# Dilated attention computed by classes of tokens modulo four: 64 by 64 blocks, two heads at a time

## The chip, the cores and the metric

One core of one Trainium2 chip runs the whole program. The metric is the device time of one execution in microseconds (us), lower is better; the kernel before was run three times.

## The reference, cut to what matters

Everything is float32. The program is two transformer blocks one after the other over 256 tokens of width 1024. The change touches one layer of the first block, dilated attention, and the tables that it reads:

```
B_WINDOWS = (128, 512, 2048)
B_DILATIONS = (1, 4, 16)
B_HEADS = 16;  B_HEAD_DIM = 64;  SEQ = 256
...
biases = [rel_bias[bucket][..., g * B_HEADS:(g + 1) * B_HEADS] ... for g ...]
...
s = einsum('birhd,bjrhd->bhrij', qb, kb) + biases[g]     # queries and keys of equal residue r only
s = where(valid, s, -inf)                                # distance in 0..window, not before token 0
p = exp(s - logsumexp(s));  o = einsum('bhrij,bjrhd->birhd', p, vb)
...
wts = softmax(stack(lses), axis=0)                       # over the three groups
o = einsum('gbqh,gbqhd->bqhd', wts, stack(outs));  return o @ w_o
```

There are three groups of 16 heads each. In group g a query attends to the keys whose distance is a multiple of the dilation: every key for group 0 (window 128), every fourth for group 1, every sixteenth for group 2. Weighting the three outputs by the softmax of their log sums is the same as one softmax over the keys of all three groups together, and the kernel computes it that way: one row of probabilities per query and head, over three stretches of keys. The bias depends on the head, the group and the distance.

## The kernel before, in words

The program is a series of stages: a feed-forward stage, a gated recurrence (`hgrn`, the reference's `_hgrn2`), another feed-forward stage, `dil` (the dilated attention), and so on. In the profiled execution `hgrn` runs from about 233 to 357 us, the feed-forward stage after it to 727, and `dil` to about 1027.

**Weights.** SyncE (queue q1, "SPq") loads each weight slice into `raw`. ScalarE copies it rounded to `whi` (L1304), VectorE computes the rest `wlo` (L1724), and TensorE multiplies by both. Only a few buffers of `raw` exist, so a load goes out when an earlier one has been read, and it is needed some microseconds later.

**Slots.** A stage with projections is cut into slots. A slot of `dil` is one product of 48 matmuls (L793 to L795 for q and v, L814 to L816 for k; also L793 for a part). Heads go in four units of four heads. A unit has nine slots: q and k for three groups (six slots), then v for three groups. The q and k slots are scaled by VectorE into `dl_t` (L1768), squared by ScalarE, summed by TensorE (L1011, L1012) and normalized. Values go through VectorE into `dl_v` (L1786).

**Attention steps.** The attention of one unit is laid into the slots of the next one, at half-slot points listed in four tables. TensorE takes the steps in the order of its program, and while it does one of them, no projection runs:

```
DL_SCORES = (13, 14, 16, 18)
DL_SCALE = (14, 15, 17, 19)
DL_TURN = (15, 17, 19, 21)
DL_PV = (19, 22)
```

For each head of a unit: SCORES (TensorE, L1056) multiplies 128 queries by 256 keys and the first 128 queries by 128 keys, for the three groups, where one head or group takes rows 0 to 63 of the array and another rows 64 to 127; VectorE adds the bias and takes the maximum (L2010); ScalarE takes the exponential (L1533) in place in `dl_S` (128 x 1152 for a head); SCALE divides by the sum (L2002 on VectorE, L2293 on GpSimd); TURN transposes nine 128 x 128 pieces (L1039) and ScalarE copies them to `dl_PT` (L1528). PV (L1024) multiplies by the values of two heads, one in columns 0 to 63 of the array, the other in 64 to 127; its result goes to `dl_oT` (L1523). Blocks of groups 1 and 2 are computed as densely as those of group 0: the bias of a distance that is not allowed is a large negative number.

**Bias tables.** The bias by distance is made in `hgrn`, where TensorE multiplies a table of zeros and ones by `rel_bias` (L994) at ticks 8, 10 and 12, ScalarE copies the result to `bias_rows` (L1496) a tick later, and ScalarE's queue (q10, "ACTq") stores it to DRAM many times over, each time shifted by a row, so that a later load finds a skewed table. Twelve stores (L1423), one for each tick from 10 on and the last three together in the last tick, each read all 128 partitions. A tick is one slot of `hgrn`: 16 ticks of projections and four of the output product (L883 to L885). Before `dil` ScalarE's queue waits for all stores, and then loads the bias of each head (L1507) two heads ahead, right after the head's exponentials.

Of the kernel before, what the change touches and what calls it, by code (L numbers as in the profile page):

```python
# [18 lines left out]
ALU = mybir.AluOpType  # L19
# [6 lines left out]
P = 128  # L26
# [22 lines left out]
SWAPPED = 1  # L49
# [16 lines left out]
def t5_bucket(dist):  # L66
# [8 lines left out]
    ("neg_mask", P), ("hg_mask", (LEVELS - 1) * P), ("swa_mask", T), ("cos", T), ("sin", T), ("onehot", GROUPS * 3 * P),  # L75
# [9 lines left out]
def constants():  # L85
# [36 lines left out]
    onehot = np.zeros((BUCKETS + 1, GROUPS, 3 * P), np.float32)  # L122
    dist = T - 1 - np.arange(3 * P)
    for g, (w, dil) in enumerate(zip(WINDOWS, DILATIONS)):
        valid = (dist >= 0) & (dist <= w) & (dist % dil == 0)
        bucket = t5_bucket(np.maximum(dist, 0))
        onehot[bucket[valid], g, np.nonzero(valid)[0]] = 1.0
        onehot[BUCKETS, g] = ~valid
# [4 lines left out]
def build_program(nc, io, upto=None):  # L133
# [87 lines left out]
    ROW = 3 * P  # L221
    REPEAT = P // HEADS
    BIAS_STORES = 4 * GROUPS
    spare = ExitStack()
    bias_rows = sb("bias_rows", [P, GROUPS, ROW], F32, spare)
    rbx = sb("rbx", [BUCKETS + 1, GROUPS * HEADS], F32, spare)
    rbx8 = sb("rbx8", [BUCKETS + 1, GROUPS * P], F32, spare)
    onehot = sb("onehot", [BUCKETS + 1, GROUPS * ROW], F32, spare)
# [64 lines left out]

    bias_dram = nc.dram_tensor("bias_by_distance", (GROUPS * HEADS * P * ROW,), F32, kind="Internal").ap()

# [90 lines left out]

    def r_of(e):

        return r[:, e % 2:e % 2 + 1, :].broadcast_to([P, 2, T])
# [63 lines left out]
    HG_BIAS = 8  # L453
# [53 lines left out]

    region = ExitStack()
# [3 lines left out]
    dl_v = sb("dl_v", [P, 2, GROUPS, T // P, 4 * HD], F32, region)  # L512
    dl_bias = sb("dl_bias", [P, 2, GROUPS, T], F32, region)
    dl_S = sb("dl_S", [P, 2, 3 * GROUPS * P], F32, region)
    dl_PT = sb("dl_PT", [P, 2, 3 * GROUPS * P], F32, region)
# [23 lines left out]
    DL_SCORES = (13, 14, 16, 18)  # L539
    DL_SCALE = (14, 15, 17, 19)  # L540
    DL_TURN = (15, 17, 19, 21)
# [23 lines left out]
    def dl_blocks(ap, keys):  # L565

        at0 = 0 if keys == T else GROUPS * T
        return ap[:, at0:at0 + GROUPS * keys].rearrange("p (g k) -> p g k", g=GROUPS)

    dl_ps = ps[:, DL_BANK:DL_BANK + 3, :].rearrange("p b n -> p (b n)")[:, 0:3 * GROUPS * P]  # L570

    def dl_paired(hd):

        return hd < HEADS - 2

    def dl_scores(hd, keys):

        at0, bank = 0 if keys == T else T, DL_BANK + (hd % 2 and dl_paired(hd))
        return ps[:, bank:bank + GROUPS, at0:at0 + keys]

    def dl_rows(a, g):

        odd = (a + (g == SWAPPED)) % 2
        return slice(HD * odd, HD * (odd + 1))
# [191 lines left out]
    def _(pe):  # L776
# [133 lines left out]
        def hgrn():  # L910
# [56 lines left out]
            for t in range(HG_TICKS):  # L967
# [20 lines left out]
                if t in HG_BIAS_AT:  # L988
# [3 lines left out]
                    else:  # L992
                        pe.wait_ge(bias_masked, 2)
                    nc.tensor.matmul(ps[:, HG_BIAS_BANK, 0:ROW], rbx8[:, P * g:P * (g + 1)], onehot[:, ROW * g:ROW * (g + 1)],  # L994
                                     start=True, stop=True).then_inc(bias_made, 1)


        def dil():
            st, e, ek = stages["dil"], reads["dil"], reads["dil"] - 1

            def steps(point):
# [11 lines left out]
                for two in dl_due(point, DL_PV):  # L1013
# [1357 lines left out]
```

## Time and profile before

| | us |
|---|---|
| median of 3 runs | 2165.11 |
| lowest and highest run | 2163.71, 2165.37 |
| span of the profiled execution | 2161.0 |
| TensorE busy, of the span | 2126.5 (98%) |
| VectorE busy | 1607.5 (74%) |
| ScalarE busy | 1307.3 (60%) |
| one unit of `dil`, 840.30 to 909.05 | 68.75 |

The profile gives no time of the profiled execution other than its span, from the first to the last instruction: the median of the runs is 4.1 us above it. "Busy" is the time in which an engine had an instruction under way. TensorE has two rows in every view: PE are the matmuls, PEld the loads of their weights, which run beside the matmul before. A float32 matmul that is not of rounded operands leaves two records. The column PEclk is the granted clock of TensorE, 1.00 being full.

### The profile page before, as it was taken

To read this page: it belongs to the slowest core of one execution; us is meant where nothing else is said; L and a number is where in the kernel's file an instruction comes from. 1 tells how busy PE (TensorE), PEld (TensorE's weight loads), DVE (VectorE), ACT (ScalarE), POOL (GpSimd) and SP (SyncE) were. 2 spreads that over 40 slices of the span, in tenths; PEclk is the share of its full clock that TensorE was granted. 3 is DMA by queue.
4 is the path that set the end of the run, shared out by engine and by line. 5 is a ranking of instruction groups with operands and counts; after the bars stand their busy time and mean duration, and the time that the engine had idled before them with its cause. 6 is when DMAs were issued, how large, how long until landed. Compare 5 with 4: busy or idle time off the path is not lost.

```text
span 2161.0 us, 39632 instructions
## 1 busy us (share of the span) xinstructions
PE 2126.5 (98%) x14203; PEld 1920.3 (89%) x14203; DVE 1607.5 (74%) x1915; ACT 1307.3 (60%) x1815; POOL 586.1 (27%) x450
## 2 busy tenths in 40 slices
PE   8999899999999999999999999999999999999998
PEld 7889899888888899999888888999888888888887
DVE  7875888886887676766887687665887688677874
ACT  6664776664665565665665566475665466456663
POOL 3431672440342000000442243000342144122430
PEclk9999999999999999999999999999999999999999
DMA  6665467666566555554566567544566566534673
GB/s 211 193 199 180 128 191 259 193 209 189 166 194 212 165 172 162 160 160 150 168 194 211 158 194 220 159 145 149 177 192 212 158 191 202 187 108 150 191 221 100
DMA packets 371157, 387.92 MB, mean 180 GB/s; under 512 B 11334, under 2 KB 366031, under 8 KB 371056
## 3 DMA queue, kind: packets, MB, share of 16 engines
q1 hardware_dynamic: 357104, 369.14, 54.9%
q10 hardware_dynamic: 13952, 17.41, 2.5%
q8 instruction: 66, 1.08, 0.2%
q14 instruction: 35, 0.29, 0.0%
HBM read 376.02 MB, written 10.49 MB: 179 GB/s over the span
## 4 chain that ended last, share of the span: by engine, by line
PE 90%; DVE 5%; ACT 3%; POOL 1%; issue 1%; DMA 0%; ACTq 0%; DVEq 0%
PE ps L839 44%; PE ps L840 23%; PE ps L793 3%; PE ps L794 3%; PE ps L795 3%; PE ps L814 2%; PE ps L815 1%; PE ps L816 1%; DVE xg L1742 1%; PE ps L883 1%; DVE wlo L1724 1%; PE ps L885 1%; PE ps L884 1%; PE ps L1056 1%; PE ps L1024 1%
## 5 line engine op out<-in xcount | busy, mean ns | idle before, releaser
L1724 DVE TENSOR_TENSOR wlo<-raw,whi 128x1024 fp32r<-128x1024 f32 (+2 forms) x652 | 883.1, 1364 | 153.7 <-ACT whi L1304 152.6
L839 PE MATMUL ps<-xg,whi 128*128 128x512 f32 x2816 | 981.8, 392 | 4.1 <-DVE xg L1742 1.9
L1304 ACT ACTIVATE whi<-raw 128x1024 fp32r<-128x1024 f32 (+2 forms) x652 | 720.6, 1113 | 190.5 <-PE ps L840 130.2
L840 PE MATMUL ps<-xg,wlo 128*128 128x256 f32 x2816 | 794.5, 282 | 0.0
L839 PEld LDWEIGHTS ps<-xg,whi 128*128 128x128 f32 x2816 | 529.2, 188 | 118.3 <-DVE xg L1742 3.9
L840 PEld LDWEIGHTS ps<-xg,wlo 128*128 128x128 f32 x2816 | 532.9, 189 | 0.2
L839 PE MATMUL ps<-hT,whi 128*128 128x512 f32 x1408 | 488.5, 390 | 0.0
L840 PE MATMUL ps<-hT,wlo 128*128 128x256 f32 x1408 | 397.1, 282 | 0.0
L839 PEld LDWEIGHTS ps<-hT,whi 128*128 128x128 f32 x1408 | 264.3, 188 | 55.4
L2235 POOL TENSOR_TENSOR gate_r<-gate,r 128x512 f32<-128x512 f32 x88 | 189.6, 2155 | 286.5 <-DVE gate L1802 286.5
L840 PEld LDWEIGHTS ps<-hT,wlo 128*128 128x128 f32 x1408 | 266.1, 189 | 0.0
L793 PE MATMUL ps<-xg,whi 128*128 128x256 f32 x576 | 164.7, 286 | 3.2 <-DVE wlo L1724 3.2
L794 PE MATMUL ps<-xg,whi 128*128 128x256 f32 x576 | 160.8, 279 | 0.0
L2240 POOL TENSOR_TENSOR hT<-h,hT 128x512 f32 x88 | 117.3, 1333 | 159.8 <-ACT hT L1357 159.8
L795 PE MATMUL ps<-xg,wlo 128*128 128x256 f32 x576 | 160.6, 279 | 0.0
L2238 POOL TENSOR_TENSOR gate_s<-gate_r,gate_s 128x512 f32<-128x512 f32 x88 | 114.9, 1306 | 155.9 <-ACT gate_s L1351 155.9
L1820 DVE SCALAR_TENSOR_TENSOR x<-ps,x 128x512 f32<-128x512 f32 x32 | 22.1, 692 | 157.1 <-PE ps L840 157.1
L1346 ACT ACTIVATE gate_e<-gate 128x512 f32<-128x512 f32 x88 | 55.7, 633 | 137.2 <-DVE gate L1802 137.2
L1806 DVE TENSOR_SCALAR gate_e<-gate_e 128x512 f32<-128x512 f32 x88 | 129.6, 1472 | 5.6 <-ACT gate_e L1346 5.6
L2227 POOL TENSOR_TENSOR acc<-acc,sq 128x512 f32<-128x512 f32 x13 | 18.2, 1401 | 369.9 <-ACT sq L1316 369.9
L793 PEld LDWEIGHTS ps<-xg,whi 128*128 128x128 f32 x576 | 108.3, 188 | 7.0 <-issue 4.9
L1311 ACT ACTIVATE xg<-x,gains 128x256 fp32r<-128x256 f32 x96 | 43.4, 500 | 110.2 <-DVE x L1822 102.1
(286 smaller groups left out, 3067.2 us busy)
## 6 DMA issues: line engine op xcount, KB each, us to landing
raw<-in_ffn_w_in SPq DMA_DIRECT2D x352, 512.0 KB, 3.5
raw<-in_ffn_w_out SPq DMA_DIRECT2D x64, 768.0 KB, 4.7
raw<-in_ffn_w_out SPq DMA_DIRECT2D x64, 640.0 KB, 4.7
raw<-in_w_kv SPq DMA_DIRECT2D x48, 512.0 KB, 3.6
raw<-in_a_w_in SPq DMA_DIRECT2D x32, 512.0 KB, 4.5
raw<-in_b_w_q SPq DMA_DIRECT2D x24, 512.0 KB, 3.8
raw<-in_sb_w_qkv SPq DMA_DIRECT2D x24, 512.0 KB, 3.9
bias_by_distance<-bias_rows ACTq DMA_DIRECT2D x12, 768.0 KB, 5.0
```

Of the source, the lines that this page charges most:

```text
L793: nc.tensor.matmul(out, whi[:, par, w], hi[:, k, :], start=k == 0 and m == 0, stop=False)
L794: nc.tensor.matmul(out, whi[:, par, w], lo[:, k, :], start=False, stop=False)
L795: mm = nc.tensor.matmul(out, wlo[:, par, w], hi[:, k, :], start=False, stop=k == total - 1 and m == 1)
L839: nc.tensor.matmul(out, whi[:, par, w], both, start=first and k == 0, stop=False)
L840: mm = nc.tensor.matmul(out[:, 0:T], wlo[:, par, w], both[:, 0:T], start=False, stop=last and k == total - 1)
L1304: nc.scalar.activation(whi[:, par, off:off + size], raw[:, 2 * par + half, :size], ACT.Copy).then_inc(hi_done, 1)
L1346: nc.scalar.activation(gate_e[:, :], gate[:, :], ACT.Exp, scale=-1.0).then_inc(gate_exp, 1)
L1724: nc.vector.tensor_tensor(wlo[:, par, off:off + size], raw[:, 2 * par + half, :size], whi[:, par, off:off + size].bitcast(F32), ALU.subtra ...
L1806: nc.vector.tensor_scalar(gate_e[:, :], gate_e[:, :], EXP_MAX, 1.0, ALU.min, ALU.add).then_inc(gate_den, 1)
L2235: nc.gpsimd.tensor_tensor(pair(gate_r[:, :]), pair(gate[:, :]), r_of(e), ALU.mult).then_inc(gr_done, 1)
L2238: nc.gpsimd.tensor_tensor(gate_s[:, :], gate_r[:, :], gate_s[:, :], ALU.mult).then_inc(gs_done, 1)
L2240: nc.gpsimd.tensor_tensor(hidden(i, 1), pair(h[:, :]), hidden(i, 0).bitcast(F32), ALU.subtract).then_inc(hT_ready, 1)
```

## The change

The tokens of a product that belongs to `dil` are written in order of their class modulo four: first tokens 0, 4, 8, ..., then 1, 5, 9, ... A group with dilation 4 or 16 then has all its allowed pairs inside four blocks of 64 by 64. Group 0 still takes 128 queries by 256 keys, now for both tiles of queries, since its class order mixes early and late tokens. A head's row of probabilities shrinks from 1152 columns of `dl_S` (768 and 384) to 768 (two tiles of 384). Groups 1 and 2 are computed as 64 x 64 matmuls in one of the four quadrants of the array, two heads together. Steps come two heads at a time.

The tables of steps, and the VectorE step for the values of groups 1 and 2 (one call in each of their slots, in place of `scaled_values`):

```
-    DL_SCORES = (13, 14, 16, 18)
-    DL_SCALE = (14, 15, 17, 19)
-    DL_TURN = (15, 17, 19, 21)
+    DL_SCORES = (13, 17)
+    DL_SCALE = (14, 18)
+    DL_TURN = (16, 20)
     DL_PV = (19, 22)
...
+        def class_values(g, u, fill):
+
+            for tile in range(2):
+                for half in range(2):
+                    rows, out = slice(HD * half, HD * (half + 1)), slice(HD * (g - 1), HD * g)
+                    op = nc.vector.tensor_scalar(dl_w[out, u % 2, 2 * tile + half, :], bank_of(fill)[rows, W2 * tile:W2 * (tile + 1)],
+                                                 r_col[rows, tile:tile + 1], None, ALU.mult)
+            op.then_inc(evac_done, 1)
```

PV:

```
-                    for g in range(GROUPS):
-                        for tile in range(2):
-                            for odd in range(2):
-                                v = dl_v[:, u % 2, g, tile, HD * (2 * c + odd):HD * (2 * c + odd + 1)]
-                                at0, n = (T * g, T) if tile == 0 else (GROUPS * T + P * g, P)
-                                mm = nc.tensor.matmul(ps[HD * odd:HD * (odd + 1), DL_OUT, T * (c + 1) - n:T * (c + 1)], v,
-                                                      dl_PT[:, odd, at0:at0 + n], start=g == 0 and tile == 0 and c == 0,
-                                                      stop=g == GROUPS - 1 and tile == 1, tile_position=(0, HD * odd), skip_group_check=True)
+                    for tile in range(2):
+                        for odd in range(2):
+                            v = dl_v[:, u % 2, tile, HD * (2 * c + odd):HD * (2 * c + odd + 1)]
+                            nc.tensor.matmul(ps[HD * odd:HD * (odd + 1), DL_OUT, T * c:T * (c + 1)], v, dl_PT[:, odd, T * tile:T * (tile + 1)],
+                                             start=c == 0 and tile == 0, stop=False, tile_position=(0, HD * odd), skip_group_check=True)
+                    for kind in range(CLASSES):
+                        at0 = OF_CLASS * kind
+                        for odd in range(2):
+                            w = dl_w[:, u % 2, kind, HD * (2 * c + odd):HD * (2 * c + odd + 1)]
+                            mm = nc.tensor.matmul(ps[HD * odd:HD * (odd + 1), DL_OUT, T * c + at0:T * c + at0 + OF_CLASS], w,
+                                                  dl_PT[:, odd, 2 * T + at0:2 * T + at0 + OF_CLASS], start=False, stop=kind == CLASSES - 1,
+                                                  tile_position=(0, HD * odd), skip_group_check=True)
```

SCORES, the part for groups 1 and 2, and the order of a pair's steps:

```
+                    def far(hds, tile):
+
+                        for g in range(1, GROUPS):
+                            for half in range(2):
+                                for hd in hds:
+                                    rows, at0 = dl_rows(hd), T * c + OF_CLASS * (2 * tile + half)
+                                    bank = DL_BANK if dl_split(hd, tile) else DL_BANK + 2 * (hd % 2) + 1 - tile
+                                    cols = (DL_TILE if dl_split(hd, tile) else dl_far(tile)) + OF_CLASS * (g - 1)
+                                    mm = nc.tensor.matmul(ps[HD * half:HD * (half + 1), bank, cols:cols + OF_CLASS],
+                                                          dl_q[rows, g, at0:at0 + OF_CLASS], dl_k[rows, u % 2, g, at0:at0 + OF_CLASS],
+                                                          start=True, stop=True, tile_position=(rows.start, HD * half))
...
+                    if odd < HEADS - 1:
+                        for tile in (1, 0):
+                            near(even, tile)
+                            near(odd, tile)
+                        far((even, odd), 1)
+                        far((even, odd), 0).then_inc(dl_scored, 2)
```

The stores and the loads of the bias tables:

```
-            def store_bias(g, quarter):
-
-                rows = REPEAT // 2
-                act.dma_start(bass.AP(bias_dram.tensor, HEADS * P * ROW * g + rows * ROW * quarter, [[4 * rows * ROW, P], [ROW, rows], [1, ROW]]),
-                              bias_rows[:, g:g + 1, :].broadcast_to([P, rows, ROW])).then_inc(bias_stored, 16)
+            def store_bias(at0, row, first, head, step):
+
+                act.dma_start(bass.AP(bias_dram.tensor, first, [[head, HEADS], [step, OF_CLASS], [1, row]]),
+                              bias_rows[0:HEADS, at0:at0 + row].unsqueeze(1).broadcast_to([HEADS, OF_CLASS, row])).then_inc(bias_stored, 16)
...
+    HG_STORE_AT = (12, 13, 14)
...
-                src = bass.AP(bias_dram.tensor, hd * P * ROW + P - 1, [[ROW - 1, P], [HEADS * P * ROW, GROUPS], [1, T]])
-                act.dma_start(dl_bias[:, hd % 2, :, :], src).then_inc((dl_bias_in0, dl_bias_in1)[hd % 2], 16)
+                arrived = (dl_bias_in0, dl_bias_in1)[hd % 2]
+                for block in range(2):
+                    near = bass.AP(bias_dram.tensor, hd * NEAR_HEAD + P * (1 + 2 * block) + OF_CLASS - 1,
+                                   [[NEAR_ROW - 1, P], [P, CLASSES], [1, OF_CLASS]])
+                    act.dma_start(dl_bias[:, hd % 2, DL_TILE * block:DL_TILE * block + T].rearrange("p (k j) -> p k j", k=CLASSES),
+                                  near).then_inc(arrived, 16)
+                far = bass.AP(bias_dram.tensor, FAR_TABLE + hd * FAR_HEAD + OF_CLASS - 1, [[FAR_STEP - 1, P], [P, 2], [1, OF_CLASS]])
+                act.dma_start(dl_bias[:, hd % 2, T:T + P].rearrange("p (g x) -> p g x", g=2), far).then_inc(arrived, 16)
```

The four stores carry as much as the twelve did, 9.4 MB: two of 16 x 64 x 896 words (3.67 MB each, at ticks 12 and 13, in pieces of 3584 bytes) and two of 16 x 64 x 256 words (1.05 MB each, at tick 14, in pieces of 1024 bytes). They read 16 partitions, one for each head. VectorE's read of the q and k products and of their factors, its and ScalarE's writes of `dl_oT`, and the writes of k's operand in the stage before are now strided.

Three places of the program's order bear on what follows. The first is TensorE in a slot of `dil`, k's product (L814 to L816) with the SCORES of one pair of heads in it and the first PV and TURN of a pair, before (`ps<-dl_k,dl_q` are SCORES, `ps<-cst,dl_S` TURN, `ps<-dl_PT,dl_v` PV):

```order
L816 MATMUL ps<-whi,xk_lo 128x256
L1056 MATMUL ps<-dl_k,dl_q 128x256 x2
L1056 MATMUL ps<-dl_k,dl_q 128x128 x2
L1056 MATMUL ps<-dl_k,dl_q 128x256 x2
L1056 MATMUL ps<-dl_k,dl_q 128x128 x2
...
L1056 MATMUL ps<-dl_k,dl_q 128x256 x2
L1056 MATMUL ps<-dl_k,dl_q 128x128 x2
...
L1039 MATMUL ps<-cst,dl_S 128x128 x9
```

In the changed program the same place reads as follows, up to its first TURN:

```order
L863 MATMUL ps<-whi,xk_lo 128x256
L1111 MATMUL ps<-dl_k,dl_q 128x256 x4
L1121 MATMUL ps<-dl_k,dl_q 64x64 x16
...
L1093 MATMUL ps<-cst,dl_S 128x128 x2
L1094 MATMUL ps<-cst,dl_S 128x128
L1093 MATMUL ps<-cst,dl_S 128x128 x2
L1094 MATMUL ps<-cst,dl_S 128x128
L1093 MATMUL ps<-cst,dl_S 128x128 x2
L1094 MATMUL ps<-cst,dl_S 128x128
L1093 MATMUL ps<-cst,dl_S 128x128 x2
L1094 MATMUL ps<-cst,dl_S 128x128
```

The second head's scores have moved up into the first head's step, twelve dense matmuls have become four dense ones and sixteen small ones, and two times nine transposes at two points have become twelve at one. The second place is PV on TensorE, before and then after:

```order
L1024 MATMUL ps<-dl_PT,dl_v 64x256 x2
L1024 MATMUL ps<-dl_PT,dl_v 64x128 x2
L1024 MATMUL ps<-dl_PT,dl_v 64x256 x2
L1024 MATMUL ps<-dl_PT,dl_v 64x128 x2
L1024 MATMUL ps<-dl_PT,dl_v 64x256 x2
L1024 MATMUL ps<-dl_PT,dl_v 64x128 x2
```

```order
L841 MATMUL ps<-xg,whi 128x256
L842 MATMUL ps<-xg,wlo 128x256
L1072 MATMUL ps<-dl_PT,dl_v 64x256 x4
L1078 MATMUL ps<-dl_PT,dl_w 64x64 x8
L840 MATMUL ps<-xk_hi,whi 128x256
```

Six dense pairs have become two dense pairs and four of 64 columns. The third place is ScalarE in `hgrn`, the copies of a table (L1496) and the stores that it issues. Before, from tick 11 on:

```order
L1304 ACTIVATE whi<-raw 128x1024
L1423 DMA bias_by_distance<-bias_rows 128x4x384
L1304 ACTIVATE whi<-raw 128x1024 x2
L1407 ACTIVATE newton<-ps,eps 128x256
L1409 ACTIVATE newton<-newton 128x256
L1485 ACTIVATE hg_v<-ps,r_col 128x256 x2
L1496 ACTIVATE bias_rows<-ps 128x384
L1423 DMA bias_by_distance<-bias_rows 128x4x384
L1304 ACTIVATE whi<-raw 128x1024 x2
```

In the changed program:

```order
L1572 ACTIVATE hg_v<-ps,r_col 128x256 x2
L1584 ACTIVATE bias_rows<-ps 128x384
L1506 DMA bias_by_distance<-bias_rows 16x64x896
L1388 ACTIVATE whi<-raw 128x1024 x2
...
L1506 DMA bias_by_distance<-bias_rows 16x64x896
L1388 ACTIVATE whi<-raw 128x1024 x2
...
L1584 ACTIVATE bias_rows<-ps 128x256
L1506 DMA bias_by_distance<-bias_rows 16x64x256 x2
```

No store goes out before tick 12 any more, and none after tick 14; all 9.4 MB are in ScalarE's queue within three ticks.

## Rows read from the trace of the kernel before

**Rows 1.** The page: busy time of each engine; the chain that ended last.
```profile
PE 2126.5 (98%) x14203; PEld 1920.3 (89%) x14203; DVE 1607.5 (74%) x1915; ACT 1307.3 (60%) x1815; POOL 586.1 (27%) x450
...
PE 90%; DVE 5%; ACT 3%; POOL 1%; issue 1%; DMA 0%; ACTq 0%; DVEq 0%
```
**Rows 2.** Windows: start:end, length, busy PE, PEld, DVE, ACT, POOL, clock, DMA share, GB/s.
```profile
297.00:331.00 34.00, 34.00 (x405) 32.38 (x404) 32.87 (x65) 25.91 (x45) 23.17 (x32) 1.00 0.66 215
331.00:357.00 26.00, 24.89 (x206) 24.37 (x206) 20.16 (x32) 14.62 (x24) 3.72 (x4) 1.00 0.84 278
357.00:726.00 369.00, 368.54 (x2124) 326.19 (x2123) 282.35 (x280) 221.97 (x292) 116.66 (x74) 1.00 0.62 194
...
840.30:909.05 68.75, 68.48 (x578) 64.28 (x578) 48.78 (x71) 43.12 (x63) 3.31 (x4) 1.00 0.54 162
```
**Rows 3.** The chain, one unit of dil: start, us on the chain, what.
```profile
840.29 1.51 PE ps L1056 x16
841.80 0.32 PE ps L814
842.83 0.12 PE ps L815
...
844.84 0.85 PE ps L1056 x8
845.69 0.32 PE ps L814
...
848.77 1.17 PE ps L1039 x9
...
874.69 0.98 PE ps L1039 x9
...
878.95 2.10 PE ps L1024 x24
881.05 0.32 PE ps L793
```
**Rows 4.** The chain in hgrn: small matmuls of 32 columns in pairs.
```profile
303.69 0.82 PE ps L953 x24
...
304.77 0.61 PE ps L953 x22
```
**Rows 5.** Groups of instructions by shape, 726 to 1030: busy, mean ns, idle before.
```profile
L2002 DVE TENSOR_SCALAR dl_S<-dl_S,dl_rcp 128x768 f32<-128x768 f32 x16 | 20.6, 1287 | 0.6
L1528 ACT ACTIVATE dl_PT<-ps 128x1152 f32<-128x1152 f32 x16 | 17.8, 1113 | 0.0
L1786 DVE TENSOR_SCALAR dl_v<-ps,r_col 128x256 f32<-128x256 f32 x24 | 10.5, 478 | 3.0 <-PE ps L816 2.8
```
**Rows 6.** DMA, 285 to 365: queues with packets, MB and share; issues.
```profile
q1 hardware_dynamic: 6842, 9.84, 39.0%
q10 hardware_dynamic: 6334, 9.44, 33.4%
```
**Rows 7.** The instructions that name bias_rows: issue ns, first and last; time to landing.
```profile
L1423 ACTq DMA_DIRECT2D bias_by_distance<-bias_rows x12: 366/366/1137, 287.8 to 352.0; - x12
...
DMA to landing us min/median/max: 3.5/5.0/13.4
```
**Rows 8.** ScalarE in the timeline, 297 to 307: a store, then a weight load awaited.
```profile
298.98 0.37 ACTq L1423 DMA_DIRECT2D bias_by_distance<-bias_rows  x1
...
304.98 1.06 ACT L1304 ACTIVATE whi<-raw 128x1024 fp32r<-128x1024 f32 x1 [3.65 <-DMA raw<-in_a_w_in]
```
**Rows 9.** The instructions of L1507, the bias loads of dil: issue, time to landing.
```profile
L1507 ACTq DMA_DIRECT2D dl_bias<-bias_by_distance x16: 366/366/512, 727.1 to 986.2; - x16
...
DMA to landing us min/median/max: 3.2/3.6/4.8
```

More of the change, by code:

```diff
@@ L563, in dl_qk_number, with dl_heads, dl_probs, dl_near @@
         return 2 * GROUPS * u + min(j, 2 * GROUPS)
[L565 to L584, printed above, removed]
+    def dl_heads(point, steps):
+        return [hd for two in dl_due(point, steps) for hd in (2 * two, 2 * two + 1)]
+    def dl_probs(ap, tile):
+        return ap[:, 0:DL_TILE] if tile else ap[:, DL_TILE:2 * DL_TILE]
+    def dl_near(tile):
+        return 0 if tile else P
+    def dl_far(tile):
+        return T if tile else 0
+    def dl_split(hd, tile):
+        return hd == HEADS - 1 and tile == 0
+    def dl_scores(hd, tile):
+        if dl_split(hd, tile):
+            return ps[:, DL_BANK:DL_BANK + 3, DL_TILE:]
+        return ps[:, DL_BANK + 2 * (hd % 2) + 1 - tile, 0:DL_TILE].rearrange("p (b n) -> p b n", b=3)
+    def dl_packed(hd):
+        return hd >= HEADS - 2
+    def dl_all_of(hd):
+        return hd - hd % 2 + 2 if dl_packed(hd) else hd + 1
+    def dl_turned_out(hd):
+        first = 2 * DL_TILE * (hd % 2) if dl_packed(hd) else 0
+        bank = DL_BANK if dl_packed(hd) else DL_BANK + 2 * (hd % 2)
+        return ps[:, bank:DL_BANK + 4 if first == 0 else DL_BANK + 3, :].rearrange("p b n -> p (b n)")[:, first:first + 2 * DL_TILE]
+    def dl_rows(hd):
+        return slice(HD * (hd % 2), HD * (hd % 2 + 1))
     region = ExitStack()
@@ L993, in hgrn @@
                         pe.wait_ge(bias_masked, 2)
-                    nc.tensor.matmul(ps[:, HG_BIAS_BANK, 0:ROW], rbx8[:, P * g:P * (g + 1)], onehot[:, ROW * g:ROW * (g + 1)],
-                                     start=True, stop=True).then_inc(bias_made, 1)
+                    for group, first, end in BIAS_PRODUCTS[g]:
+                        at0 = first - BIAS_PRODUCTS[g][0][1]
+                        mm = nc.tensor.matmul(ps[:, HG_BIAS_BANK, at0:at0 + end - first], rbx8[:, P * group:P * (group + 1)], onehot[:, first:end],
+                                              start=True, stop=True)
+                    mm.then_inc(bias_made, 1)
         def dil():
@@ L1040, in steps @@
                     tr.then_inc(dl_turned, 1)
[L1041 to L1042 removed]
+                for two in dl_due(point, DL_SCORES):
+                    u, c = divmod(two, 2)
                     pe.wait_ge(dl_qkd, 2 * GROUPS * (u + 1))
[L1044 to L1059 removed]
@@ new lines, in steps, with near @@
+                    if two:
+                        pe.wait_ge(dl_PTd, 2 * two)
+                    def near(hd, tile, half=None):
+                        rows, first = dl_rows(hd), T * c
+                        queries = dl_q[rows, 0, first + P * tile:first + P * (tile + 1)]
+                        if half is None:
+                            out, keys = ps[:, DL_BANK + 2 * (hd % 2) + 1 - tile, dl_near(tile):dl_near(tile) + T], dl_k[rows, u % 2, 0, first:first + T]
+                        else:
+                            out, keys = dl_scores(hd, tile)[:, 1 + half, :], dl_k[rows, u % 2, 0, first + P * half:first + P * (half + 1)]
+                        return nc.tensor.matmul(out, queries, keys, start=True, stop=True, tile_position=(rows.start, 0))
@@ L2362 @@
     arrays = {name: np.ascontiguousarray(inputs[name]) for name in INPUTS}
-    for name in ("b_w_q", "w_kv"):
-        arrays[name] = swapped_heads(arrays[name])
     arrays["consts"] = constants()
```

209 lines of the change are left out of this document (116 added, 93 removed).

## The prediction

> **What bounds the kernel now.** I read the page first: TensorE is busy for 98% of the span, and 90% of the chain that ended last is its matmuls [rows 1]. Then the windows by stage: in one unit of `dil` TensorE is busy 68.48 of 68.75 us, while VectorE has 48.78 and ScalarE 43.12 [rows 2]. So in `dil` a microsecond that TensorE doesn't work is a microsecond of the span, until another engine becomes late. Third the chain of one unit, which shows what an attention step costs there [rows 3]. Last the DMA, since the change gathers the stores of the tables: in `hgrn` from 297 to 331 us TensorE is busy throughout and the DMA engines 0.66 of the time, from 331 to 357 it is 0.84 [rows 2].
>
> **What a step costs before.** A step lies between projection matmuls that follow each other every 0.12 us; the first matmul behind a step has 0.32 on the chain [rows 3]. So a SCORES step of 16 records costs 1.51 + 0.32 - 0.12 = 1.71 us and one of 8 records 0.85 + 0.32 - 0.12 = 1.05. The longer one is the shorter one plus one pair of 256-column and one pair of 128-column matmuls, each in two records: 2 x 384 = 768 columns of a pair for 0.66 us, which is 0.86 ns a column, and 1.05 - 0.66 = 0.39 us stay as the fixed cost of a step. PV: 2.10 + 0.32 - 0.12 = 2.30, of which three groups of 2 x 384 columns are 1.98 and 0.32 fixed. TURN: four in a unit, 1.17 us for the first and 0.98 for the last, 4.45 together [rows 3]. A unit has two SCORES steps of each length (5.52), four TURN (4.45) and two PV (4.40, since one of the two runs on into a TURN): 14.4 of its 68.75 us.
>
> **What it costs after.** SCORES for a pair of heads is one step: four 256-column matmuls, two at a time, are 2 x 2 x 256 x 0.86 ns = 0.88 us. Then 16 matmuls of 64 columns in quadrants, two records each, so 8 turns if four run together. By the column a turn is 64 x 0.86 = 55 ns; the smallest matmuls of the trace, 32 columns in pairs, take 0.82 us for 12 pairs and 0.61 for 11, 68 and 55 ns each [rows 4]: there is a floor near these. I take 70 ns: 0.56 us. If four don't run together but two and two, a turn is 2 x 55 to 2 x 60 ns, 0.96 us at most. Fixed 0.39, and 0.1 for the change of array mode within the step, of which no row here shows the size (bounds 0 and 0.2). Sum 1.93 us (1.71 to 2.43) in place of 1.71 + 1.05 = 2.76: 0.83 saved (0.33 to 1.05), eight pairs: 6.6 us (2.6 to 8.4). TURN: 12 transposes at one point in place of two times nine, at 0.98/9 to 1.17/9 each 1.31 to 1.56, I take 1.45; two in a unit are 2.9 against 4.45, 1.55 saved, four units: 6.2 (5.3 to 7.3). PV: 2 x 512 columns for the two tiles of group 0 (0.88), four pairs of 64 columns (8 turns of 55 to 70 ns, 0.44 to 0.56), 0.32 fixed: 1.70 against 2.20 on average, 0.5 saved (0.4 to 0.6), eight: 4.0. Together 16.8 us less TensorE work in `dil` (12 to 20), all on the path as long as the other engines keep up.
>
> The Trainium skill, page "TensorEngine Tiling (Array Packing)", says that the 64 x 64 tiles of the array work independently of each other and that a change of the tile mode drains the array. By it the four quadrants overlap and the step is near my 1.93; the trace shows only two tiles at once, so no row here shows four.
>
> **The other engines in dil.** VectorE: the values of groups 1 and 2 take four instructions on 64 partitions in place of two on 128. At 478 ns each [rows 5], if a half costs as much as a whole, that is 0.96 us more in 2 of 9 slots, 1.9 a unit. Against it the scaling of the probabilities goes from 768 to 384 columns, 1287 ns to about 650, four times a unit: 2.5 less. ScalarE's copy to `dl_PT` goes from 1152 to 768 columns, 1113 to about 750 ns [rows 5]. The strided reads could cost at most as much again for the q and k slots; with 20 us idle in a unit [rows 2] this hides. Nothing added. The bias of a head is loaded by three DMAs of 256-byte pieces, 80 packets for an engine in place of 24. Packets of the main queues took 0.39 x 80 us x 16 / 6842 = 73 ns on average [rows 6], so 56 more are 4 us at most on top of the 3.6 us of now [rows 9]. The load goes out two heads, four half slots or about 11 us, ahead: hidden. Its issues are 3 x 0.37 us [rows 9] on ScalarE's queue in place of one, behind exponentials, beside 25 us idle: nothing. Were this cover gone, 0.7 us for each of 16 heads would show, 12 us; it is not near that.
>
> **The stores in hgrn.** The bytes are the same. All of ScalarE's queue between 285 and 365 us moved 9.44 MB in 33.4% of 80 us, 26.7 us of engine time, 2.2 for one of the twelve stores [rows 6]. A near store of 3.67 MB is then 10.4 us. Before, only ticks 12 to 15, four stores, lay in 297 to 331; now all twelve's worth does: 8 x 2.2 = 18 us more against 0.34 x 34 = 11.6 us in which the DMA engines idle there [rows 2]. About 6 us of transfers don't fit, and weight loads are behind them. That this hurts can be seen: the store issued at 298.98 was followed by a weight load whose copy (L1304) waited 3.65 us and then ran at 304.98 [rows 8]. From 331 on 13 us of transfers are gone, so some comes back. Bounds: 0, if the loads pass between the packets in time, and 12, if each of the two near stores costs what is left of its 10.4 us behind the lead of a load, about 6. I take 5.
>
> **Sum.** -16.8 + 5 = -11.8. The profiled execution's span is 2161.0, and the median is 4.1 above it; against the span the sum gives 2149.2, against the median 2153.3. I forecast 2153.
>
> **Rival B, stores that are slow by themselves: slower.** The twelve stores read 128 partitions, the four read 16 neighbouring ones, and no row shows a store from so few. In the trace the DMA engines serve both queues in turn, so a slow store packet also holds the weight loads that share its engine. If such a store takes k times as long as one of now, the stores need 26.7k us from 298 on. At k = 3 that is 53 us more, against about 16 us idle till 357 (11.6 + 0.16 x 26) and 0.38 of each later microsecond [rows 2], of which some 6 are of use before the stores end: loads slip by 53 - 22 = 31 us, minus 16.8 gives 2179. At k = 4: 80 - 16 - 16 = 48, gives 2196. At k = 2: 27 - 16 = 11, still a gain of 6. It decides from k = 2.3 on. For it: no row rules it out, and [rows 7] show a store that took 13.4 us where the median is 5.0, so stores can be held up. Against it: a DMA engine might go on with loads while a store packet waits; the packets are larger (3584 bytes), and what limits now are the engines.
>
> The Trainium skill, "SBUF — State Buffer", section "Door 1: The DMA port swizzle", says that neighbouring partitions share a few of 16 ports, and gives 104 GB/s for 16 partitions against 328 for 128. By this rule k would be about 3.2, a near store 35 us, and the time about 2180. It is the strongest voice against the change; the trace has nothing that agrees or disagrees.
>
> **Rival S, the steps turn into waits: no change.** Two heads at a time make the work between two points double: at point 17 SCORES needs both copies of `dl_PT` of TURN at 16, 2 x 0.75 us behind a TURN of 1.45, within a half slot of 2.8 us, so 0 to 0.5 us are missing. If TensorE waits 1 us a pair, 8 us are lost, and with quadrants that don't overlap 3 more: -16.8 + 11 + 5, about 2164 (2158 to 2167). Against it: 20 us of VectorE and 25 of ScalarE idle in a unit.
>
> **How the numbers follow.** Forecast 0.48, its own range 2143 (20 saved, nothing lost) to 2162 (12 saved, 9 lost); B 0.39; S 0.13. The point is the forecast's. Up to 2162 alone would hold only about 0.55, so the range reaches to 2200, past k = 4, and leaves out little. 0.2% is 4.3 us, about what can be told from no change: faster than 2160.8 is nearly all of the forecast, a third of S and the mild end of B, 0.54; within it most of the rest of S, 0.09; slower 0.37.
>
> **What would show it.** A unit of `dil` 64.5 us instead of 68.75; SCORES steps of 1.9 us; no new wait of TensorE's steps. In `hgrn` the near stores land after 10 to 15 us (B: 30 and more), and ScalarE's wait for `raw` is a few us (B: tens). Were the quadrants serial, the small matmuls of a step would take 1 us and more; were S right, TURN or SCORES would show idle time before them.

## The result and the profile after

The changed kernel takes 2206.55 us (median of 5 runs, 2206.38 to 2207.32), the kernel before 2165.05 (5 runs): ratio 1.0198, 95% interval 1.0187 to 1.0208. It is 41.5 us slower, where 12 us faster was forecast. The profiled execution has a span of 2204.6 us, against 2161.0: 43.6 apart, since the profiled execution of the kernel before was 4.1 us shorter than its median and that of the changed kernel 2.0.

The page of the changed kernel, with the rows that answer to [rows 1]:

```profile
PE 2119.5 (96%) x14287; PEld 1912.3 (87%) x14287; DVE 1618.0 (73%) x1931; ACT 1301.9 (59%) x1815; POOL 586.0 (27%) x450
...
PE 81%; DVE 8%; ACT 4%; DMA 3%; issue 2%; POOL 1%; another core or an unknown queue 1%; ACTq 1%; DVEq 0%; SPq 0%
```

TensorE has 7 us less to do, and its share of the chain has fallen from 90% to 81%: there are new waits, on DMA (3%) and on VectorE (5% to 8%). The windows say where, in the columns of [rows 2]:

```profile
300.00:407.00 107.00, 62.38 (x587) 59.15 (x586) 45.93 (x85) 34.68 (x57) 23.60 (x31) 0.78 0.97 166
407.00:776.00 369.00, 366.88 (x2110) 324.41 (x2110) 286.11 (x285) 225.17 (x297) 116.82 (x74) 1.00 0.61 189
...
893.01:959.37 66.36, 64.83 (x598) 60.78 (x598) 51.33 (x75) 41.64 (x63) 3.31 (x4) 1.00 0.56 163
```

The work that took the 60 us from 297 to 357 now takes 107. The DMA engines are busy for 0.97 of that time, but move only 166 GB/s, where 0.84 busy moved 278 before [rows 2]. The feed-forward stages behind it are as long as before, and a unit of `dil` is 66.36 us, only 2.4 shorter than 68.75. So `hgrn` lost some 50 us and `dil` gave 10 back. From the first write of `hg_raw` to the first sum of squares of `dil` the program takes 581.4 us in place of 528.4: 50.3 of these 53.0 lie in `hgrn`, 2.7 between its last matmul and that sum.

What `hgrn` waits for, in ScalarE's timeline (a row's last bracket is the idle time before it and what ended it), and then the rows on the stores that answer to [rows 7]:

```profile
312.79 0.33 ACTq L1506 DMA_DIRECT2D bias_by_distance<-bias_rows  x1
338.49 1.06 ACT L1388 ACTIVATE whi<-raw 128x1024 fp32r<-128x1024 f32 x1 [24.01 <-DMA raw<-in_a_w_in]
357.43 1.06 ACT L1388 ACTIVATE whi<-raw 128x1024 fp32r<-128x1024 f32 x1 [17.89 <-DMA raw<-in_a_w_in]
...
362.08 9.80 ACTq L1506 DMA_DIRECT2D bias_by_distance<-bias_rows  x2
```

```profile
L1506 ACTq DMA_DIRECT2D bias_by_distance<-bias_rows x4: 309/326/9453, 300.0 to 362.4; - x4
...
DMA to landing us min/median/max: 25.8/38.1/64.1
```

Two weight loads come 24 and 18 us late, and a third wait is inside the issue of the last two stores (the row with x2, 9.80 us together): one of them takes 9.45 us, in which ScalarE does nothing else. A store lands after 26 to 64 us, where the small ones took 3.5 to 13.4. The DMA view from 304 to 330 us, in which the first near store is under way and from 313 on the second stands behind it, gives the price of a piece (queue: packets, MB, share of the 16 engines):

```profile
q10 hardware_dynamic: 720, 2.58, 94.0%
q1 hardware_dynamic: 318, 0.33, 3.6%
```

0.94 x 26 us x 16 / 720 = 543 ns for a piece of 3584 bytes, so 16 engines write 106 GB/s. Before, in the same window, it was:

```profile
q1 hardware_dynamic: 1736, 3.26, 39.4%
q10 hardware_dynamic: 1584, 2.36, 26.2%
```

0.262 x 26 x 16 / 1584 = 69 ns for 1536 bytes, 357 GB/s. Byte for byte a store piece is 3.4 times dearer. And the weight loads on the same engines get fewer than one piece through for every two of these: 318 pieces in 26 us, where they got 1736. The three loads issued in that window landed after 53 to 54 us.

In `dil`, the waits of TensorE's sequencer and the chain of one q slot (start, us on the chain, what):

```profile
PEld ps L1061 <- DVE dl_sq_lo L2155: 13.3, 24, 1.9
```

```profile
939.51 1.08 DVE dl_t L1875
940.73 0.43 issue
941.16 0.62 ACT dl_sq_hi L1641
941.80 0.70 DVE dl_sq_lo L2155
942.55 0.50 PE ps L1061
943.05 0.23 PE ps L1062
```

All 24 sums of squares now wait for their operand. The chain from one product to its sum runs through VectorE's scaling into `dl_t`, two squares on ScalarE and a subtraction on VectorE, and the scaling, now strided, takes 1.08 us:

```profile
L1875 DVE TENSOR_TENSOR dl_t<-ps,r 128x512 f32<-128x512 f32 x24 | 25.8, 1076 | 16.0 <-PE ps L842 16.0
L2109 DVE TENSOR_SCALAR dl_S<-dl_S,dl_rcp 128x384 f32<-128x384 f32 x16 | 17.4, 1087 | 0.6
```

Before, the same scaling took 0.69 us and two of the 24 sums waited.

### The profile page after: what moved, and what is told of

It reads as the page before. It is cut to its first block, busy times and chain, and to the rows that moved or that the text cites. A ratio compares the mean times of both kernels' runs of the same rounds, so it can differ in the third digit from the quotient of the medians.

```text
span 2204.6 us, 39831 instructions
## 1 busy us (share of the span) xinstructions
PE 2119.5 (96%) x14287; PEld 1912.3 (87%) x14287; DVE 1618.0 (73%) x1931; ACT 1301.9 (59%) x1815; POOL 586.0 (27%) x450
## 3 DMA queue, kind: packets, MB, share of 16 engines
q8 instruction: 66, 1.08, 0.2%
## 4 chain that ended last, share of the span: by engine, by line
PE 81%; DVE 8%; ACT 4%; DMA 3%; issue 2%; POOL 1%; another core or an unknown queue 1%; ACTq 1%; DVEq 0%; SPq 0%
PE ps L886 43%; PE ps L887 23%; PE ps L840 2%; PE ps L842 2%; PE ps L841 2%; DMA raw<-in_a_w_in 2%; DVE wlo L1814 1%; PE ps L861 1%; PE ps L862 1%; PE ps L863 1%; DVE xg L1832 1%; DVE dl_t L1875 1%; DMA raw<-in_a_w_out 1%; PE ps L930 1%
## 5 line engine op out<-in xcount | busy, mean ns | idle before, releaser
L887 PEld LDWEIGHTS ps<-xg,wlo 128*128 128x128 f32 x2816 | 532.9, 189 | 0.2
L842 PEld LDWEIGHTS ps<-xg,wlo 128*128 128x128 f32 x576 | 108.7, 189 | 4.5 <-issue 4.5
```

The costliest lines, as they stand in the source:

```text
L842: mm = nc.tensor.matmul(out, wlo[:, par, w], hi[:, k, :], start=False, stop=k == total - 1 and m == 1)
L887: mm = nc.tensor.matmul(out[:, 0:T], wlo[:, par, w], both[:, 0:T], start=False, stop=last and k == total - 1)
```

## Experiments

"Spread" means in what follows that the stores read all 128 partitions, "cut" that each near store is issued as four of 0.92 MB, and "contiguous" that VectorE's scaling has no strides. Medians are of 4 to 10 runs each. The ratio is to runs of the kernel before beside them, whose median was 2165.05 for the first row and 2163.5 to 2164.0 for the others.

| kernel | us | ratio to before, 95% |
|---|---|---|
| changed kernel | 2206.55 | 1.0198 [1.0187, 1.0208] |
| stores spread | 2169.03 | 1.0023 [1.0013, 1.0032] |
| stores from every eighth partition | 2170.64 | 1.0032 [1.0022, 1.0043] |
| contiguous, stores as changed | 2199.27 | 1.0161 [1.0144, 1.0178] |
| kernel before, its stores from partitions 0 to 15 | 2199.56 | 1.0162 [1.0145, 1.0179] |
| spread, contiguous | 2161.65 | 0.9990 [0.9981, 0.9999] |
| spread, cut, at eight ticks | 2157.22 | 0.9972 [0.9962, 0.9982] |
| spread, cut, at the old ticks | 2159.82 | 0.9983 [0.9974, 0.9993] |
| cut, at eight ticks, from partitions 0 to 15 | 2198.36 | 1.0156 [1.0139, 1.0173] |
| cut in 32, sixteen neighbours at a time | 2187.43 | 1.0112 [1.0095, 1.0129] |
| spread, cut, at eight ticks, contiguous | 2149.30 | 0.9936 [0.9922, 0.9949] |
| the same, all scaling of `dl_S` on VectorE | 2149.44 | 0.9938 [0.9923, 0.9953] |

### Which partitions a store reads

First the changed kernel with the same four stores at the same ticks, read from 128 partitions. VectorE lays the factors so that each head's row comes out in eight partitions side by side, and each of them serves eight table rows:

```
-                act.dma_start(bass.AP(bias_dram.tensor, first, [[head, HEADS], [step, OF_CLASS], [1, row]]),
-                              bias_rows[0:HEADS, at0:at0 + row].unsqueeze(1).broadcast_to([HEADS, OF_CLASS, row])).then_inc(bias_stored, 16)
+                each = OF_CLASS // REPEAT
+                act.dma_start(bass.AP(bias_dram.tensor, first, [[head, HEADS], [step * each, REPEAT], [step, each], [1, row]]),
+                              bias_rows[:, at0:at0 + row].unsqueeze(1).broadcast_to([P, each, row])).then_inc(bias_stored, 16)
```

> The changed kernel, its four stores at the same ticks and of the same bytes and pieces, but read from all 128 partitions (each head's row lies in eight partitions, and each of them serves eight of the 64 table rows). Theory P (16 neighbouring partitions give a store only a part of the rate): a piece of 3584 bytes takes about 140 to 200 ns in place of 535, a near store lands within 12 to 20 us in place of 39 to 64, hgrn and the start of the next stage come back to within 0 to 12 us of before, time 2155 to 2170. Rival Q (large pieces, all issued within three ticks, starve the weight loads whatever they read): landing stays over 25 us and the time over 2185.

It took 2169.03 us: 37.5 of the 41.5 us are gone with nothing but the partitions changed, so theory P holds for the larger part and rival Q falls. The DMA window from 304 to 330 us again:

```profile
q10 hardware_dynamic: 1569, 5.57, 83.4%
q1 hardware_dynamic: 1214, 1.65, 17.2%
```

A piece now takes 0.834 x 26 x 16 / 1569 = 221 ns, 2.5 times less, and the loads get 1214 pieces through in place of 318. But 221 is above the 140 to 200 that theory P expected, a near store still landed only after 26.8 us at worst, and ScalarE waited 14.6 us in two waits for weights:

```profile
ACT whi L1388 <- DMA raw<-in_a_w_in: 14.6, 2, 8.1
```

Then 16 partitions once more, but eight apart, with the same layout:

```
-                              bias_rows[0:HEADS, at0:at0 + row].unsqueeze(1).broadcast_to([HEADS, OF_CLASS, row])).then_inc(bias_stored, 16)
+                              bias_rows[0:P:REPEAT, at0:at0 + row].unsqueeze(1).broadcast_to([HEADS, OF_CLASS, row])).then_inc(bias_stored, 16)
```

> The changed kernel, but the stores read 16 partitions that are eight apart (0, 8, ... 120) in place of 0 to 15. Theory P (what counts is which partitions, not how many): pieces of 3584 bytes in 250 to 300 ns, a near store in 20 to 30 us, time 2172 to 2190. Rival F (what counts is that there are few, 16): as the changed kernel, 535 ns a piece and 2204 to 2209. The Trainium skill, SBUF, Door 1, maps these 16 to eight ports where 0 to 15 are four: by it the rate doubles.

2170.64 us: rival F falls. That there are 16 costs almost nothing (1.6 us over 128 of them), that they are neighbours costs 36. In the DMA window:

```profile
q10 hardware_dynamic: 1449, 5.14, 88.0%
q1 hardware_dynamic: 1077, 1.18, 12.7%
```

A piece takes 253 ns, 2.15 times less than 543. The time came out a little under the range that I had worked out for it. The expected doubling of the rate, which was the rule of the Trainium skill, "SBUF — State Buffer", "Door 1: The DMA port swizzle", is what the trace shows. The 543 ns of 16 neighbours, 106 GB/s, agree with the 104 GB/s that the same section of the Trainium skill gives.

The mirror of it is the kernel before, whose twelve small stores stay at their ticks but read partitions 0 to 15. This leaves the right rows out of the tables; only its time counts:

```
-                act.dma_start(bass.AP(bias_dram.tensor, HEADS * P * ROW * g + rows * ROW * quarter, [[4 * rows * ROW, P], [ROW, rows], [1, ROW]]),
-                              bias_rows[:, g:g + 1, :].broadcast_to([P, rows, ROW])).then_inc(bias_stored, 16)
+                act.dma_start(bass.AP(bias_dram.tensor, HEADS * P * ROW * g + rows * ROW * quarter, [[4 * rows * ROW * REPEAT, HEADS], [4 * rows * ROW, REPEAT], [ROW, rows], [1, ROW]]),
+                              bias_rows[0:HEADS, g:g + 1, :].broadcast_to([HEADS, REPEAT * rows, ROW])).then_inc(bias_stored, 16)
```

> The kernel before, its twelve stores at their ticks with pieces of 1536 bytes as they are, but each read from partitions 0 to 15 only (so that the tables hold wrong rows). Theory P: a piece takes 200 to 250 ns in place of 65, a store 6 to 8 us of the DMA engines' time, twelve of them 80 to 95 us where 27 were; weight loads wait, time 2180 to 2205. Rival Q (large pieces in few ticks): nothing changes, 2163 to 2168.

2199.56 us, 35.6 us slower than before, within what theory P expected. In the same DMA window a piece of 1536 bytes takes 0.609 x 26 x 16 / 1220 = 208 ns, 3.0 times the 69 of before:

```profile
q10 hardware_dynamic: 1220, 1.82, 60.9%
```

So the slow partitions do the harm alone, with small pieces and spread over ten ticks.

### How much a store carries, and when it goes

The other part: spread, with the near stores cut into eight of 0.92 MB, one for each tick from 12 on:

```
+                if HG_STORE_AT <= t < HG_STORE_AT + 8:
+                    nth = t - HG_STORE_AT
+                    store_bias(0, NEAR_ROW, NEAR_SECOND * (nth // 4), NEAR_HEAD, NEAR_ROW, nth % 4, 4)
+                if t in HG_FAR_AT:
```

> The four stores from 128 partitions, and the two near ones cut into eight of 0.92 MB, one for each tick from 12 to 19, the far ones at ticks 16 and 18; the scaling still strided. Theory P2 (what was left in hgrn after the stores read all partitions, two waits for weights of 14.6 us together, comes from 3.67 MB going out at once): no wait for raw longer than some 4 us, hgrn as long as before, and dil 9.6 us shorter, time 2153 to 2160. Rival (what is left is the share of the writes, since the bytes now go out within eight ticks in place of ten): 2164 to 2169.

2157.22 us, as theory P2 expected. Its stores land after 5.6 to 12.8 us, and no wait for `raw` is longer than 1.4 us. That left open whether the cut or the later ticks did it. So the same cut stores, four at tick 12, four at tick 13 and the far ones at tick 14:

```
-                if HG_STORE_AT <= t < HG_STORE_AT + 8:
-                    nth = t - HG_STORE_AT
+                for nth in {12: range(4), 13: range(4, 8)}.get(t, ()):
```

> The stores from 128 partitions, the near ones cut into eight of 0.92 MB, but issued four at tick 12 and four at tick 13, the far ones at tick 14, as the changed kernel issues its four; scaling strided. Theory T (the rest of the wait in hgrn comes from how much is queued at once, not from the size of one store): as with four uncut stores, waits for raw of 12 to 18 us in sum, 2166 to 2171. Rival C (the cut itself lets the loads pass): 2155 to 2160.

2159.82 us. Theory T fell, and rival C held: the cut alone brought 9.2 us, the ticks 2.6 more. The DMA window of this version, and then of the one at eight ticks:

```profile
q10 hardware_dynamic: 2007, 6.62, 68.5%
q1 hardware_dynamic: 1610, 3.07, 32.1%
```

```profile
q10 hardware_dynamic: 933, 3.15, 46.3%
```

The packets of these two windows include short ones (a store leaves 16 records of 4 bytes, and at the end of the first window a far store has begun), so the bytes are the better divisor: 0.685 x 26 x 16 x 3584 / 6.62 MB = 154 ns for the bytes of a near piece, and by the same sum 219 at eight ticks, where the uncut store has 223. All stores together, from 285 to 425 us, in the order changed kernel, spread, cut at the old ticks, cut at eight ticks:

```profile
q10 hardware_dynamic: 4160, 9.44, 58.0%
q10 hardware_dynamic: 4160, 9.44, 24.4%
q10 hardware_dynamic: 4256, 9.44, 18.7%
q10 hardware_dynamic: 4256, 9.44, 23.4%
```

That is 81, 34, 26 and 33 us of the 16 engines, where the twelve stores of before took 27. So the cut at the old ticks did make the pieces cheaper. But the fastest of these versions pays nearly the uncut price: there the gain is in how little is queued ahead of a load at one time. The cut also changes which partitions are read near each other in time, since a partition serves two rows of a store in place of eight. That may be why the pieces of a burst are cheaper when cut, but no run shows it by itself, nor why they are dearer again at eight ticks.

The cut and the ticks without the spread:

```
-                              bias_rows[:, at0:at0 + row].unsqueeze(1).broadcast_to([P, each, row])).then_inc(bias_stored, 16)
+                              bias_rows[0:HEADS, at0:at0 + row].unsqueeze(1).broadcast_to([HEADS, each, row])).then_inc(bias_stored, 16)
```

> The stores cut and one for each tick from 12 to 19, far ones at 16 and 18, as in the version that read 128 partitions, but read from partitions 0 to 15 as in the changed kernel; scaling strided. Theory P: the slow pieces (about 535 ns) need some 80 us of the DMA engines however they are spread, and the stores run on behind their ticks, so 35 to 48 us over the 2157 of the version with 128 partitions, 2192 to 2205. Rival T2 (spread over eight ticks the slow stores leave room for the loads): under 2175.

2198.36 us, as theory P expected: with slow pieces (56.5% of the same 140 us, 79 us of the engines) the cut and the ticks bring 8 us and no more. The waits have moved to a later place, 37.4 us at the first loads of the next stage.

Last, all 128 partitions, but 16 neighbours in each store:

```
+                for k in range(REPEAT):
+                    act.dma_start(bass.AP(bias_dram.tensor, first + each * step * k, [[head, HEADS], [step, each], [1, row]]),
+                                  bias_rows[HEADS * k:HEADS * (k + 1), at0:at0 + row].unsqueeze(1).broadcast_to([HEADS, each, row])).then_inc(bias_stored, 16)
```

> The changed kernel, its layout of bias_rows and its ticks as they are, but each of the four stores cut into eight: the first writes rows 0 to 7 of each head from partitions 0 to 15, the next rows 8 to 15 from partitions 16 to 31, and so on, so that all 128 partitions are read, sixteen neighbours at a time, in 32 small stores. Scaling strided. Theory M (what counts is which partitions the 16 DMA engines read at the same moment): pieces of 3584 bytes stay near 400 to 540 ns and the time over 2190. Rival A (it is enough that the whole set of stores reads all partitions, or that the stores are small): pieces of 140 to 250 ns, as in the cut version that spread its reads, and 2157 to 2172.

2187.43 us, between the two and in neither range. By the bytes a piece took 0.697 x 26 x 16 x 3584 / 4.12 MB = 252 ns on average, less than half of 543. Several of the small stores, from different partitions, are under way at once, which may be the reason; no run shows it. Another cost came in, which neither theory had:

```profile
ACT whi L1388 <- issue: 42.6, 3, 19.2
```

ScalarE's copies of weights waited 42.6 us behind its own issues of stores (32 of them, up to 3.9 us each). So this run doesn't decide between M and A; it shows that many stores at once on ScalarE's queue stop ScalarE itself.

### The strided scaling

q's operand is written in class order as k's is, and the factors `r` are copied once into class order:

```
-            across = r[:, e % 2, :].rearrange("p (i k) -> p k i", k=CLASSES).unsqueeze(1).broadcast_to([P, 2, CLASSES, OF_CLASS])
-            nc.vector.tensor_tensor(classes(out), source, across, ALU.mult).then_inc(evac_done, 1)
+            nc.vector.tensor_tensor(pair(out), pair(source), rc[:, e % 2:e % 2 + 1, :].broadcast_to([P, 2, T]), ALU.mult).then_inc(evac_done, 1)
```

> The changed kernel with its stores as they are, but q's operand is written in class order too and the factors r are copied once into class order, so that VectorE reads and writes dl_t without strides. Theory D (in dil the strided scaling, 1.08 in place of 0.69 us, makes TensorE wait at the sum of squares, 24 times about 0.4 us): scaling back to 0.69 us, the sum step from 1.0 to 0.6 us, a unit 64.0 us in place of 66.35, time 2195 to 2199. Rival (the two-heads order makes the wait, not the stride): the unit stays over 66 and the time at 2205 to 2208.

2199.27 us, 7.3 less and 0.3 above what theory D expected; the rival falls. The scaling is back at 690 ns, and a unit is 64.07 us, with TensorE busy in all of it:

```profile
827.47:891.54 64.07, 64.07 (x598) 60.78 (x598) 48.97 (x75) 41.65 (x63) 3.31 (x4) 1.00 0.58 169
```

With the spread stores:

> Both edits: four stores read from 128 partitions, and VectorE's scaling of q and k without strides. If the two causes are independent, the gains add: 2169.0 less the 7.3 us that the second gave, 2162 (2160 to 2164), just under the kernel before. If the waits in hgrn hid part of the second, less.

2161.65 us, within what was expected. The gains add to within 0.1 us (37.5 and 7.3 by themselves, 44.9 together), so the two causes are independent.

### All of it, and GpSimd's part in the scaling

> All three edits. Theory: what the step costs of the prediction said of TensorE in dil is then left by itself, 18.8 us of a unit's steps in four units: 2165 less 17 to 19 plus 0 to 3 for the later stores, 2146 to 2152. Rival, the two heads in one step put waits elsewhere in dil: over 2155.

2149.30 us, ratio 0.9936 [0.9922, 0.9949]: this is the fastest version, 14.2 us under the kernel before. A unit's chain begins like that of [rows 3]:

```profile
841.90 1.06 PE ps L1115 x8
842.96 0.62 PE ps L1125 x32
843.59 0.32 PE ps L865
```

Here L1115 are the matmuls of group 0 and L1125 those in quadrants. Not all is gained: the first sum of squares of `dil` comes at 744.51 us in place of 738.24. The traces show where the 6.3 us lie. 1.2 are there before `hgrn` writes its first `hg_raw` (211.0 in place of 209.8), where the version of the next edit, the same program up to `dil`, has nothing; that much differs between executions. The rest divides at the last matmul of `hgrn`:

| from the first `hg_raw` | to the last matmul of `hgrn` | from there to the first sum |
|---|---|---|
| before | 146.5 | 381.9 |
| changed kernel | 196.8 | 384.6 |
| spread | 161.1 | 382.6 |
| spread, cut, at the old ticks | 152.7 | 382.7 |
| spread, cut, at eight ticks | 147.3 | 384.6 |
| this version | 148.4 | 385.1 |
| its next edit | 147.2 | 384.7 |

The two versions whose spread stores all go out by tick 14 lose 0.7 to 0.8 us behind `hgrn`; more than that the strided writes of k's operand can't cost there. The three at eight ticks issue their last store some 4 us before the last matmul of `hgrn` and lose 2.7 to 3.2, and ScalarE waits 4.2 to 4.8 us for the first weights of the feed-forward stage. So what is left lies in front of `dil`, and most of it points to the late stores.

In its last edit VectorE scales both tiles of the probabilities and GpSimd none:

```
+                    for tile, scaled_one in ((1, dl_sc1), (0, dl_sc0)):
+                        own = dl_probs(dl_S[:, hd % 2, :], tile)
+                        nc.vector.tensor_scalar(own, own, dl_rcp[:, hd % 2, tile:tile + 1], None, ALU.mult).then_inc(scaled_one, 1)
```

> As the one with all three edits, but VectorE scales both tiles of the probabilities and GpSimd none. In the changed kernel VectorE's scaling of 384 columns took 1087 ns beside GpSimd's of 828 ns, and before 1287 ns for 768 columns: 828 + 259 and 828 + 459, as if VectorE first waited for GpSimd's whole instruction. If so, each of VectorE's two takes about 260 ns without GpSimd, 520 in place of 1087. Since nothing in dil waits for VectorE any more, the time stays within 1 us. Rival: 384 columns take about 650 ns by themselves, and two of them 1300.

2149.44 us, unchanged as expected. Neither number for the instruction came out:

```profile
L2113 DVE TENSOR_SCALAR dl_S<-dl_S,dl_rcp 128x384 f32<-128x384 f32 x32 | 12.0, 418 | 0.6
```

Alone it takes 418 ns, not 260 nor 650. Beside GpSimd's it took 1087. VectorE does both tiles by itself in 2 x 418 = 836 ns, less than its half took with GpSimd's help.

## Why the prediction was wrong

**The stores.** The step that failed is the choice between "I take 5" and rival B. The rival's mechanism is what happened: the stores of 16 neighbouring partitions are slow by themselves, and hold the weight loads on the same engines. All stores together took 81 us of the engines (58.0% of 140 us) in place of 27, so its k was 3.0 (a near piece by itself 3.4: 543 ns, against 69 x 3584 / 1536 = 161). For k = 3 it gave 31 us lost and a time of 2179; about 50 were lost in `hgrn`, and the time is 2206.5. So the rival had the mechanism, and its sum was 20 us short: it let the loads use what the engines have idle, but while the slow stores run they are busy for 0.95 to 1.02 of the time and the loads get 3.6% of it. By replacing only the partitions, 37.5 us of the loss went (35.6 the other way, on the kernel before). What misled me was the sentence against it, that a DMA engine might go on with loads while a store piece waits: 318 load pieces beside 720 store pieces in 26 us, 94.0% and 3.6% of the engines' time, show that it doesn't. The rule of the Trainium skill that the prediction cites, "SBUF — State Buffer", "Door 1: The DMA port swizzle", gives 104 GB/s, and the trace shows 106. With no row for or against an unseen access pattern, the only evidence was the one with a number; I set it below half.

**The scaling.** "The strided reads could cost at most as much again ... this hides. Nothing added" is the second step that failed. The cost itself was within my bound (1.08 for 0.69 us). The cover was wrong: I weighed 0.4 us against 20 us of idle time of VectorE in a unit, but the instruction is a link in a chain with a fixed place at its end, the sum of squares, for which TensorE waits. It cost 0.4 us in each of the 24 q and k slots, 9.3 by that count and 7.3 to 7.9 by the runs.

**TensorE's steps.** These held. From the rows of the trace a SCORES step costs 1.06 + 0.62 + 0.32 - 0.12 = 1.88 us (I had 1.93), a TURN of twelve 1.31 (1.45), PV 1.67 (1.70). The sixteen quadrant matmuls take 0.62 us in 32 records, so four run together in 78 ns where I had 70: they overlap. Together the steps of a unit are 9.7 us in place of 14.4; 4.7 of 68.75 is what the contiguous version shows (64.07), 18.7 in four units where I had 16.8. Two ends of the range were added up wrongly (the low ends of the three savings give 11, not 12, and 20 saved give 2145, not 2143); nothing hangs on them.

**The large stores as such.** The 5 us (0 to 12) for a gathered burst at full speed had a real mechanism and a fair size where the pieces are at full speed: the cut and spread version at the old ticks takes 7.0 us longer than the kernel before from the first `hg_raw` to the first sum of squares. The uncut one, whose pieces still cost more than those of before, takes 15.3 longer, past my bounds.

**The other engines.** Rival S did not come in the form that I gave it: no SCORES, TURN or PV step waits for VectorE or ScalarE. VectorE's scaling of the probabilities was mis-sized (1087 ns, not 650), at no cost once the q and k chain was short. The values of a class cost 482 ns for half the partitions, as expected, and the bias loads were hidden.

**The loss of TensorE's clock.** In `hgrn` TensorE stands nearly idle for 34 us, and its granted clock is 0.50 there, the lower of its two levels (1.2 of 2.4 GHz). When it is busy again throughout, the first 2 us are still at 0.50:

```profile
323.00:357.00 34.00, 2.02 (x11) 1.73 (x9) 1.23 (x1) 1.06 (x1) 0.00 (x0) 0.50 1.01 129
360.00:362.00 2.00, 2.00 (x26) 1.35 (x25) 1.17 (x3) 1.94 (x4) 0.14 (x1) 0.50 1.02 186
```

The mean from 300 to 407 is 0.78. The work there took it 62.4 us busy in place of 58.9 [rows 2], for 587 records in place of 611: some 3.5 of the 50 us, which no term of mine had.

## What to carry to other kernels

When a DMA is rewritten to read or write fewer partitions, price it by which partitions the 16 engines touch at once, not by its bytes: 16 neighbours wrote at 106 GB/s here, 16 that lie eight apart at 227, and every other transfer on those engines slows with them. Cut a large background store into parts that the foreground can wait for (here 0.92 MB, 2157 to 2160 us in place of 2169), but not into so many that the queue blocks the engine that issues them (here 32, 2187 us). Idle time of an engine covers an added cost only where the instruction isn't a link between two instructions of the engine that bounds: follow its result to whoever waits for it.

## What the runs showed of the hardware

- A store of 3584-byte pieces from partitions 0 to 15 takes 543 ns a piece, from 0, 8, ... 120 it takes 253, from all 128 it takes 221 in one large store. Cut in four it takes 154 when the parts are issued at once, and 219 when they are spread over eight ticks; the reason of that difference stays open.
- Issuing a DMA is not always short: with stores queued up, an issue on ScalarE's queue took up to 9.45 us (0.31 to 0.33 for the others), and the engine did nothing else in that time.
- VectorE's scaling of 128 x 384 in place takes 418 ns alone and 1087 ns beside GpSimd's on the neighbouring columns, which takes 828. The Trainium skill, "SBUF — State Buffer", "Who interferes with whom", says that VectorE, in its modes with two ports, shares a port pair with GpSimd, which whoever issues first holds for its whole instruction while the other waits. The direction agrees; 828 + 418 is more than 1087, though, so here part of the two overlaps.
- VectorE's multiplication of 128 x 512 elements takes 690 ns with contiguous operands and 1076 when an operand is read with a step of four elements.
